# Weighing attention values with one head's high and low parts side by side: two matrix products for three, and two halves to add

## The reference, cut to what matters

```python
h = _rmsnorm(x, norm1_g[l]); proj = h @ w_in[l]
fox = _forgetting_attention(...)        # softmax(q k^T * scale + c_q - c_k), causal, then  p @ v
sb  = _stick_breaking_attention(...)    # exp(log_sigmoid(z) + suffix sums), strictly causal, then  a @ v
mix = concat(_rmsnorm(_from_heads(fox), g_fox[l]), _rmsnorm(_from_heads(sb), g_sb[l]))
x = x + mix @ w_out[l]
x = x + _moe(_rmsnorm(x, norm2_g[l]), ...)
```

## Time and profile before

| | |
|---|---|
| median of three executions | 1458.0 us (1457.93 to 1458.38) |
| the profiled execution | 1459.92 us, of which the span of the profile is 1458.0 us |
| PE | busy 1427.6 us (98%) |
| DVE | busy 1312.9 us (90%) |
| ACT | busy 1103.7 us (76%) |
| chain of work that ended last | PE 87%, DVE 7%, ACT 3%, DMA 2%, issue 1% |

### The profile page before, as it was taken

How to read it: one execution, slowest core, us unless ns; L and a number is a source line. 1 busy time by engine, 2 the same in 40 slices (tenths; PEclk the granted TensorE clock), 3 DMA queues, 4 the chain that set the end, 5 groups by cost and what they waited for, 6 DMA issues and landing times.

```text
span 1458.0 us, 22359 instructions
## 1 busy us (share of the span) xinstructions
PE 1427.6 (98%) x7068; PEld 1161.3 (80%) x7068; DVE 1312.9 (90%) x1529; ACT 1103.7 (76%) x1348; POOL 381.4 (26%) x177
## 2 busy tenths in 40 slices
PE   9999999999999999999999999999999999999995
PEld 7777787787888888888888888888888888888884
DVE  5778766679999999999999999999999999999997
ACT  5668554467888888888888888888888888888884
POOL 3000000050443333333333333333333333333222
PEclk9999999999999999999999999999999999999998
DMA  8021022469999999999999999999999999999963
GB/s 260 14 74 59 29 87 77 115 238 392 406 394 394 396 386 388 384 385 381 382 370 390 376 385 385 375 369 388 373 379 381 375 380 374 378 382 384 366 219 126
DMA packets 98317, 451.88 MB, mean 310 GB/s; under 512 B 11427, under 2 KB 23715, under 8 KB 65506
## 3 DMA queue, kind: packets, MB, share of 16 engines
q1 hardware_dynamic: 90962, 434.68, 77.7%
q0 software_dynamic: 7312, 16.63, 5.0%
HBM read 440.99 MB, written 18.48 MB: 315 GB/s over the span
## 4 chain that ended last, share of the span: by engine, by line
PE 87%; DVE 7%; ACT 3%; DMA 2%; issue 1%; POOL 0%; SPq 0%; ACTq 0%; POOLq 0%; DVEq 0%
PE zpair L2223 47%; PE bank L2223 24%; PE bank L1923 2%; PE bank L1811 2%; PE bank L1813 2%; PE bank L1812 2%; PE bank L2173 1%; PE bank L2181 1%; DVE stage_lo L1221 1%; DVE lbuf L1301 1%; DMA x_scratch<-qk,sidx 1%; PE zpair L2192 1%; DVE pt_lo L1310 1%; DVE lbuf L1297 0%; DVE cols L1318 0%
## 5 line engine op out<-in xcount | busy, mean ns | idle before, releaser
L1221 DVE TENSOR_TENSOR stage_lo<-ring,stage_hi 128x1024 fp32r<-128x1024 f32 x796 | 944.6, 1219 | 40.2 <-ACT stage_hi L788 12.3
L788 ACT CAST stage_hi<-ring 128x1024 fp32r<-128x1024 f32 x796 | 828.2, 1054 | 167.8 <-PE zpair L2223 133.7
L2223 PE MATMUL zpair<-stage_hi,act_hi 128*128 128x512 f32 x1024 | 322.6, 396 | 0.3 <-DVE act_lo L1626 0.3
L668 POOL COPY sidx<-gtab 96x1 int32 (+1 forms) x31 | 231.3, 7461 | 346.3 <-ACT qk L1107 346.3
L2223 PE MATMUL zpair<-stage_hi,act_lo 128*128 128x512 f32 x1024 | 316.8, 391 | 0.0
L2223 PE MATMUL zpair<-stage_lo,act_hi 128*128 128x512 f32 x1024 | 315.9, 390 | 0.5 <-DVE stage_lo L1221 0.5
L2223 PEld LDWEIGHTS zpair<-stage_lo,act_hi 128*128 128x128 f32 x1024 | 192.1, 188 | 42.8 <-DVE stage_lo L1221 1.4
L2223 PEld LDWEIGHTS zpair<-stage_hi,act_lo 128*128 128x128 f32 x1024 | 192.2, 188 | 41.1
L2223 PEld LDWEIGHTS zpair<-stage_hi,act_hi 128*128 128x128 f32 x1024 | 187.2, 188 | 42.9 <-issue 7.2
L2223 PE MATMUL bank<-stage_hi,act_hi 128*128 128x512 f32 x510 | 159.8, 395 | 0.0
L2223 PE MATMUL bank<-stage_lo,act_hi 128*128 128x512 f32 x510 | 157.1, 389 | 0.0
(11 more groups left out here) (307 smaller groups left out, 1429.0 us busy)
## 6 DMA issues: line engine op xcount, KB each, us to landing
ring<-in_w SPq DMA_DIRECT2D x384, 1024.0 KB, 8.9
ring<-in_w_in SPq DMA_DIRECT2D x12, 1024.0 KB, 5.2
ring<-in_w_out SPq DMA_DIRECT2D x4, 1024.0 KB, 5.2
xs_all<-in_x SPq DMA_DIRECT2D x4, 512.0 KB, 5.8
ring<-in_x SPq DMA_DIRECT2D x4, 512.0 KB, 3.6
tn_scratch<-qk SPq DMA_DIRECT2D x4, 512.0 KB, 2.8
x_scratch<-ring SPq DMA_DIRECT2D x4, 512.0 KB, 3.6
ring<-x_scratch SPq DMA_DIRECT2D x4, 512.0 KB, 5.9
```

Of the source, the lines that this page charges most:

```text
L668: nc.gpsimd.tensor_copy(sidx[:], gtab[:, i:i + 1] if isinstance(i, int) else gtab[:, bass.ds(i, 1)]).then_inc(sidx_copied, 1)
L788: nc.scalar.copy(dst, src).then_inc(split_hi, 1)
L1221: nc.vector.tensor_tensor(dst, src, hi_ap.bitcast(F32), ALU.subtract).then_inc(split_lo, 1)
L2223: mm = pe.matmul(bank[b0 + h][:], w[:, k, :], m[:, j % STAGES, h * BANK:(h + 1) * BANK], start=start and w is T_hi and m is stage_hi, stop ...
```

## The change

`v_hi` and `v_lo` become one tile, `v_parts`, with four groups of 64 columns: high part of head 0, low part of head 0, low part of head 1, high part of head 1. `weigh` takes two neighbouring groups of one head as its 128 columns: `obank[m]` then holds, in one half of its rows, the high values' product and in the other half the low values' product, both by `pt_hi` and by `pt_lo`. That is two matmuls where there were three, 16 for a pair instead of 24. The two halves of the rows must then be added across partitions: ScalarE copies the low half to the other head rows of a tile `mixed` (the former `f_max`), and VectorE adds the high half in place (`mix_sum`). From then on one instruction of 128 rows handles both heads: high part (`mix_round`), low part (`mix_rest`), squares in place (`mix_square`), sum of squares (`add_squares`). The last pair, fox pair 3, keeps three products and the old evacuation (`mix_last`).

```diff
-        v_hi = over("v_hi", [P, 2, TT, P], F32R, qk_at + 16384)
-        v_lo = over("v_lo", [P, 2, TT, P], F32R, qk_at + 20480)
+        v_parts = over("v_parts", [P, 2, TT, 4, HD], F32R, qk_at + 16384)
...
+            def mix_move(kind, c):
+                at = pair_at(kind, c)
+                act.wait_ge(*((pvs_done, TT * (c + 1)) if kind else (pvf_done, c + 1)))
...
+                for m in range(2):
+                    half, other = slice(64 * m, 64 * m + 64), slice(64 - 64 * m, 128 - 64 * m)
+                    nc.scalar.copy(mixed[half, :], obank[m][other, :]).then_inc(mix_copied, 1)
+            def mix_round(kind, c):
+                act.wait_ge(mix_added, pair_at(kind, c) + 2)
+                nc.scalar.activation(hi_t[:, c, :], mixed, ACT.Copy, scale=...).then_inc(mix_copied, 2)
+            def mix_square(kind, c):
+                act.wait_ge(mix_added, pair_at(kind, c) + 4)
...
+                nc.scalar.activation(mixed if c else sq_sum[kind], mixed, ACT.Square).then_inc(mix_sq, 2)
...
-                if s > STICK and s % TT == 1 and s > STICK + TT:
-                    mix_evac(0, (s - STICK - TT) // TT)
+                if s > STICK + TT and s % TT:
+                    (mix_move, mix_round, mix_square)[s % TT - 1](0, (s - STICK - TT) // TT)
+                elif TT < s < STICK + TT and s % TT == 3:
+                    mix_square(1, s // TT - 1)
...
-                if TT < s < STICK + TT and s % TT == 1:
-                    mix_evac(1, s // TT - 1)
+                if TT < s < STICK + TT and s % TT in (1, 2):
+                    (mix_move, mix_round)[s % TT - 1](1, s // TT - 1)
...
+            def mix_sum(kind, c):
+                for m in range(2):
+                    half = slice(64 * m, 64 * m + 64)
+                    dve.wait_ge(mix_copied, pair_at(kind, c) + m + 1)
+                    nc.vector.tensor_tensor(mixed[half, :], obank[m][half, :], mixed[half, :], ALU.add).then_inc(mix_added, 1)
+            def mix_rest(kind, c):
+                dve.wait_ge(mix_copied, pair_at(kind, c) + 4)
+                nc.vector.scalar_tensor_tensor(out=lo_t[:, c, :], in0=mixed, ...).then_inc(mix_added, 2)
...
-                if s > STICK + TT and s % TT == 2:
-                    mix_lo_part(0, (s - STICK - TT) // TT)
+                if s > STICK + TT and s % TT:
+                    (mix_sum, mix_rest, add_squares)[s % TT - 1](0, (s - STICK - TT) // TT)
+                elif TT < s < STICK + TT and s % TT == 3:
+                    add_squares(1, s // TT - 1)
...
-                if TT < s < STICK + TT and s % TT == 1:
-                    mix_lo_part(1, s // TT - 1)
+                if TT < s < STICK + TT and s % TT in (1, 2):
+                    (mix_sum, mix_rest)[s % TT - 1](1, s // TT - 1)
...
-                        for w, x in ((v_hi, pt_hi), (v_hi, pt_lo), (v_lo, pt_hi)):
+                        if ph == 2 * PAIRS - 1:
+                            ways = ((0, pt_hi), (0, pt_lo), (2, pt_hi))
+                        else:
+                            ways = ((2 * m, pt_hi), (2 * m, pt_lo))
```

More of the change, by code:

```diff
@@ L124, in out_filled, with pair_at @@
     return max(0, streamed(q) - FILLS)
+def pair_at(kind, c):
+    return 4 * (PAIRS * (1 - kind) + c)
 def out_done_at(j):
@@ L919, in mix_evac, with mix_last @@
+            def mix_last():
+                at = pair_at(0, PAIRS - 1)
+                act.wait_ge(pvf_done, PAIRS)
                 for m in range(2):
                     half = slice(64 * m, 64 * m + 64)
[L921 to L926, removed]
@@ L927, in mix_evac @@
-                last = not kind and c == PAIRS - 1
+                    nc.scalar.activation(fox_hi[half, PAIRS - 1, :], obank[m][half, :], ACT.Copy,
+                                         scale=gmix[half, PAIRS - 1:PAIRS]).then_inc(mix_copied, 1)
+                act.wait_ge(sq_added, 3 + PAIRS - 2)
                 for m in range(2):
                     half = slice(64 * m, 64 * m + 64)
[L930 to L933, removed]
+                    act.wait_ge(mix_added, at + m + 1)
+                    nc.scalar.activation(mixed[half, :], obank[m][half, :], ACT.Square).then_inc(mix_sq, 1)
@@ L1339, in pt_lo_part @@
                                         pt_hi[:, :, i:4 * i + 1:3, :].bitcast(F32), ALU.subtract).then_inc(pt_lo_r, 1)
[L1341 to L1345, removed]
+            def mix_sum(kind, c):
                 for m in range(2):
                     half = slice(64 * m, 64 * m + 64)
[L1348 to L1356, removed]
-                    ins = nc.vector.tensor_tensor(sq_sum[kind][:], sq_sum[kind][:], sq_new[:], ALU.add).then_inc(sq_added, 1)
-                    if c == PAIRS - 1:
-                        dve.wait_ge(sq_added, 3 * (2 - kind))
-                        dve.sem_inc(sq_summed, 1)
@@ new lines, in mix_sum @@
+                    dve.wait_ge(mix_copied, pair_at(kind, c) + m + 1)
+                    nc.vector.tensor_tensor(mixed[half, :], obank[m][half, :], mixed[half, :], ALU.add).then_inc(mix_added, 1)
+            def mix_rest(kind, c):
+                hi_t, lo_t = (stick_hi, stick_lo) if kind else (fox_hi, fox_lo)
+                dve.wait_ge(mix_copied, pair_at(kind, c) + 4)
+                nc.vector.scalar_tensor_tensor(out=lo_t[:, c, :], in0=mixed, scalar=gmix[:, 4 * kind + c:4 * kind + c + 1],
+                                               in1=hi_t[:, c, :].bitcast(F32), op0=ALU.mult, op1=ALU.subtract).then_inc(mix_added, 2)
@@ new lines, in add_squares @@
+            def add_squares(kind, c):
+                if c == 0:
+                    return
+                if c > 1:
+                    dve.wait_ge(sq_added, 3 * (1 - kind) + c - 1)
+                dve.wait_ge(mix_sq, pair_at(kind, c) // 2 + 2)
+                nc.vector.tensor_tensor(sq_sum[kind][:], sq_sum[kind][:], mixed[:], ALU.add).then_inc(sq_added, 1)
+                if c == PAIRS - 1:
+                    dve.wait_ge(sq_added, 3 * (2 - kind))
+                    dve.sem_inc(sq_summed, 1)
@@ L1921, in weigh @@
                     for m in range(2):
[L1922 to L1923 removed]
+                        if ph == 2 * PAIRS - 1:
+                            ways = ((0, pt_hi), (0, pt_lo), (2, pt_hi))
+                        else:
+                            ways = ((2 * m, pt_hi), (2 * m, pt_lo))
+                        for n, (g, x) in enumerate(ways):
+                            mm = pe.matmul(obank[m][:, kb * P:S], v_parts[:, ph % 2, kb, g:g + 2, :].rearrange("p g d -> p (g d)"),
                                            x[:, m, 4 * kb:3 * kb + TT, :].rearrange("p i q -> p (i q)"),
[L1925 removed]
+                                           start=kb == 0 and n == 0, stop=kb == TT - 1 and n == len(ways) - 1, skip_group_check=True)
                 return mm
@@ L1980, in sums @@
                 pe.wait_ge(sq_summed, 2 - kind)
-                pe.wait_ge(mix_lo, 2 * PAIRS * (2 - kind))
+                pe.wait_ge(mix_added, pair_at(1, PAIRS) if kind else pair_at(0, PAIRS - 1) + 2)
                 for t in range(TT):
```

47 lines of the change are left out of this document (32 added, 15 removed).

## The result

The changed kernel takes 1469.7 us (median of 5 runs, 1468.0 to 1470.3), the kernel before 1458.0 (median of 5, 1457.3 to 1459.9). The ratio is 1.0076, with a 95% interval of 1.0065 to 1.0086: slower by 11.7 us (9.5 to 12.5 by the interval), where +7.0 was forecast. The profiled execution of the changed kernel took 1469.71 us with a span of 1467.9, that of before had a span of 1458.0: 9.9 us in the traces. (The profiled execution of before was itself 1.9 us above its median.)

A forecast was written before the change was run, and what follows sets the result against it. PE sets the pace, with DVE and ACT close behind in the stick steps. Products -8.8, waits +12.2, pair 3 -1.2 make +2.2; clock +4.8 makes +7.0 on 1458.0: 1465.0 us, range 1456 to 1470.

The forecast's parts named there:

- the forecast by itself: All three waits occur and the clock falls behind two or three of them: 1462 to 1468 us, 52%.
- more is late: Rival: stalls at the upper bound of 15 us and a clock term of 6.6 us, giving 1469.6 us; 10%.
- products: Seven pairs' products on PE: 16 matmuls instead of 24 save 8.8 us, passed on to all engines.
- waits behind the squares: Stick steps 6, 10, 14: ACT's squares wait for `mix_rest`, delaying PE by 4.2 + 4.0 + 4.0 = 12.2 us.
- clock: PE's granted clock falls behind each of the three new idle times: 4.8 us, bounds 0 and 6.6.
- pair 3: Steps 17 to 19: work leaves DVE's step 17, so PE's wait for `pt_lo` goes: -1.2 us.
- evacuation's own work, stick pairs: DVE gets about 0.6 us more per pair, said to fit into its idle time: counted as nothing.
- evacuation, fox pairs: Sums stand where DVE waited for PE, squares where ACT waits: counted as nothing, bounds -1.2 and +0.9 us.
- The rival of products that don't get shorter: Matmul pace is set by something other than their number, and the waits stand: 1473.8 us; 3%.
- The rival of a hidden wait: PE finds `stick_exp` ready in time in steps 6, 10 and 14: 1448.0 us, or 1452 if partly hidden; 13%.
- the clock holds: Rival: PE's clock does not fall behind the new waits, so the sum is 2.2 us: 1460.2 us; 22%.
- the rows at 322 us agree with it: Low clock behind PE's 1.73 us wait at 322.47 us, 1.7 us of missing work, taken as support for the clock term.

The follow-up runs named there:

- e3: Kernel before, with the third product (low values with `pt_hi`) left out in the first seven pairs and the old evacuation kept: 1450.7 us, ratio 0.9941.
- e1: Changed kernel with ACT's squares of stick pairs 0 to 2 moved behind the step's exponentials instead of ahead of `pt_hi`: 1452.3 us, ratio 0.9960.
- e2: Changed kernel in its order, with throwaway matmuls filling PE's three long waits in steps 7, 11 and 15: 1463.8 us, ratio 1.0036.
- e5: Changed kernel with the squares of pair 1 alone moved to the end of step 11: 1462.8 us, ratio 1.0025.
- e7: e6 with ACT rounding ahead of the softplus tail and squaring where it rounded, DVE adding halves and taking the rest earlier: 1454.0 us, ratio 0.9967.
- e6: e1 with DVE's sum of squares of pairs 1 and 2 put off to steps 13 and 17: 1451.2 us, ratio 0.9946.
- e8: e7 with 14 throwaway matmuls on PE in the wait for the gathered rows near 318 us: 1454.1 us, ratio 0.9965.

## Why the prediction was right, and where its sizes were off

Direction, mechanism and places held; the time of 1469.7 is inside the range of 1456 to 1470, but only 0.3 us from its upper end, and outside the 1462 to 1468 that the prediction gave to the forecast by itself. It also meets the 1469.6 of the rival "more is late", by chance: that rival had 15 us of waits and 6.6 of clock, the runs show 11.5 and 5.8, and what is over came from terms that both had at nothing. Each term, in us, by the intervals (their sum is 10.1):

| term | forecast | measured | by |
|---|---|---|---|
| products | -8.8 | -9.0 | e3 less before |
| waits behind the squares | +12.2 | +11.5 | after less e1, without the clock |
| clock | +4.8 | +5.8 | after less e2 |
| pair 3 | -1.2 | -1.1 | e1 less e3, interval 3 to 4 |
| evacuation's own work, stick pairs | 0 | +2.45 | e1 less e3, first three |
| evacuation, fox pairs | 0 (-1.2 to +0.9) | +0.5 | e1 less e3, last three |

- *The products.* Right, also in that the saving is passed on in full. A product of 16 took 2.76 to 2.79 us on the chain where it follows a wait, against "about 2.5" forecast, which is the figure without one (2.50 us at 203.57 on the chain). The rival of products that don't get shorter falls with e3.
- *The order.* Right in place and size; e1 and e5 show it by taking the waits away, all and one. The rival of a hidden wait falls: the squares came 3.75 us late, as the row of `k_lo` had said.
- *Pair 3.* Right, and shown twice: PE's wait for `pt_lo` is gone in the changed kernel and e1, and comes back with 1.14 us in e7, when DVE gets work of step 17 back.
- *The clock.* The rival "the clock holds" falls. The term was sized 1.0 us small, and that it came so near is partly luck, as two larger errors cancel. The forecast took 1.7 us of missing work for each wait (1.4 of it counted for the third), from a single case; missing were 1.7, 3.4 and 5.2 us, twice as much in all. But they cost 1.5, 2.1 and 2.2 us. Part of the rest lies in the waits themselves: in the window of 162 to 164 us PE still stands in the third wait and the clock is already at 0.55, which is 0.9 us of missing work that costs nothing. Another part takes the place of waits that PE has at the full clock: the 0.61 and 1.00 us for the values' low part in e2 are gone here. Behind the third wait about 1 us stays unexplained.
- *The evacuation's own work.* This is the step that was mis-sized. The prediction put it at nothing with the words "As busy time alone that fits into its idle time". DVE's idle time in the stick steps was an average over 125 us; between `k_lo` and the product it works almost without a gap, as the prediction itself said a paragraph later to explain why nothing is caught up. The change puts `mix_rest` into that stretch for each of the three pairs, and the sum of squares for pairs 1 and 2. e6 shows the sum, 0.6 us for each of two pairs. What is left by e6 less e3 is 0.66 us in interval 0 to 1, 0.2 in 1 to 2 and 0.3 in 2 to 3. In interval 0 to 1 the two traces fit `mix_rest`. DVE's timeline in e1, then in e3:

```profile
89.50 0.69 DVE L1308 SCALAR_TENSOR_TENSOR k_lo<-bank,k_hi 128x512 fp32r<-128x512 f32 x1
90.10 0.74 DVE L1389 SCALAR_TENSOR_TENSOR stick_lo<-f_max,cols,stick_hi 128x512 fp32r<-128x512 f32 x1
90.76 0.75 DVE L1347 TENSOR_TENSOR pt_lo<-bank,pt_hi 128x256 fp32r<-128x256 f32 x2
...
90.27 0.69 DVE L1271 SCALAR_TENSOR_TENSOR k_lo<-bank,k_hi 128x512 fp32r<-128x512 f32 x1
90.87 0.75 DVE L1310 TENSOR_TENSOR pt_lo<-bank,pt_hi 128x256 fp32r<-128x256 f32 x2
```

  From `k_lo` to `pt_lo` it is 1.26 us in e1 and 0.60 in e3: 0.66 us more, as much as the interval. No run moved `mix_rest` alone, so its share is read from the traces and not shown by an experiment; the 0.2 and 0.3 us were not parted.

By the intervals the sum missed 3.1 us: 2.45 + 0.5 + 1.0 + 0.1, less the 0.2 and 0.7 by which products and waits came out better. The medians lie 11.7 us apart, another 1.6 above the intervals' 10.1; the profiled execution of before, from which its intervals come, was 1.9 us above its median.

## What to carry to other kernels

An instruction that is put into the middle of an engine's fixed order and waits for another engine can cost what all instructions behind it are late, so find its operand's instruction in the timeline of the other engine and read the lateness there before placing it; here moving one instruction of ACT, in three pairs, behind the step's exponentials turned +0.8% into -0.4%. "It fits into the idle time" has to be checked in the stretch between the instruction and the next hand-over, not in the engine's busy share. After such a wait the low clock adds to the price; throwaway matmuls give that part back (5.8 of 17.3 us here), the right order gives back all of it, though not the evacuation's own 2.45 us.

## What the runs showed of the hardware that was not expected

- The low clock lasted differently behind the same wait: three windows of 0.84, 0.50 and 0.81 in one execution, 0.50, 0.50, 0.50 and 0.97 in another, both behind 4.79 us; about 8 us behind one of 4.61 us, under matmuls that followed one another without a gap.
- In the attention loop it fell behind a wait of 2.78 us in e7 and not behind one of 2.79 us at the same place in e8, and behind none of the waits up to 1.3 us.
- Between the attention loop and the experts it also fell where PE waits for nobody for long. In e3, e6 and e8 this is near 302 to 304 us (1.85 us busy of 2 in the window ahead of it or at its start), in e1 near 304, in e7 near 317 behind a wait of only 1.02 us (at 316.51 us), and in the changed kernel, where no wait of PE from 296 to 326 us is over 0.25 us, near 322:

```profile
320.00:322.00 2.00, 1.85 (x21) 1.69 (x21) 1.83 (x11) 0.99 (x2) 0.40 (x1) 1.00 0.15 59
322.00:324.00 2.00, 2.00 (x20) 1.55 (x19) 1.86 (x8) 1.79 (x3) 0.40 (x1) 0.66 1.04 317
324.00:326.00 2.00, 2.00 (x17) 1.81 (x15) 1.17 (x4) 2.00 (x3) 0.00 (x0) 0.50 0.97 369
```

  No edit touched that part, and the cause stays open. So the earlier trace rows were weaker evidence than the prediction took them for, its "the rows at 322 us agree with it" too: that the fall there came from the wait of 1.73 us is not shown. How much of the spread of 1.0 (e2) to 4.8 us (e5) between runs of one kernel comes from such stretches is open as well.
- One instruction of 128x512 on ACT or DVE took 0.57 to 0.75 us, one of 64x512 about the same (two squares 1.21 us in the earlier trace rows, the two copies 1.19 in e1, `f_max` L938): halving the rows of an instruction saved nothing.
